# Reordering the matmuls, the copies and the DMA issues ahead of the scan in the mixer of a second block

## The reference, cut to what matters

```python
h = rms_norm(x, norm_mix_g);  p = h @ w_in
q, pc, pr = split(p)                       # 256, 768, 1536 columns
# memory attention: 4 heads of 64 over 256 rows kh, vh of the memory
s  = einsum('bqhd,bmhd->bhqm', qh, kh) * 64 ** -0.5
o_att = einsum('bhqm,bmhd->bqhd', softmax(s), vh)
# convolution: 31 taps along time for each of 384 channels, layer norm, silu
u = val * sigmoid(gate);  o_conv = silu(layer_norm(conv(u, conv_w) + conv_b))
# rwkv7, forward and backward: low-rank products for decay w, rate a, gate g
w = exp(-0.606531 * sigmoid(w0[d] + tanh(wd) @ decay_up[d]))      # rank 64, d = 0, 1
a = sigmoid(a0[d] + ad @ iclr_up[d])                              # rank 64, d = 0, 1
g = sigmoid(gd) @ gate_up                                         # rank 128
bonus[d] = sum(r * k_d * r_k, over a head's 64 channels) * v
state = state * w + (state @ -kk) (kk * a) + v k_d;  y = state @ r    # the scan
x = x + concat(o_att, o_conv, (group_norm(y) + bonus) * g) @ w_out
```

## Time and profile before

| what | value |
|---|---|
| time, median of 3 runs | 1654.49 us (1652.68 to 1655.73) |
| the profiled execution: span | 1657.7 us |
| PE busy, of the span | 1361.3 us (82%) |
| DVE, ACT, POOL busy | 423.9, 278.8, 128.0 us |
| mean granted clock of TensorE | 0.896 |
| chain that ended last, by engine | PE 53%, DMA 41% |

### The profile page before, as it was taken

The page is one execution under the profiler, slowest core; times in us unless marked ns, Lnnn a source line. Parts: engine busy times, 40 slices in busy tenths (PEclk is TensorE's granted clock), DMA queues, the critical chain, the costliest instruction groups (busy, mean ns, idle before and its releaser), DMA issues.

```text
span 1657.7 us, 26953 instructions
## 1 busy us (share of the span) xinstructions
PE 1361.3 (82%) x11688; PEld 766.4 (46%) x11688; DVE 423.9 (26%) x892; ACT 278.8 (17%) x626; POOL 128.0 (8%) x276
## 2 busy tenths in 40 slices
PE   5999999999999877877778689887987577566775
PEld 4756876787763323322223278676432122122221
DVE  1012135531273222222222244653520000000001
ACT  0201213551011111110111113331111100000001
POOL 4000013000000000000000004112000000000000
PEclk9999989999999999889898889967988878787679
DMA  9865381466469999999999691300979999999997
GB/s 347 269 171 208 110 299 57 166 238 238 178 254 396 426 429 427 429 429 429 427 429 427 288 330 51 95 3 4 375 313 429 428 429 427 430 428 428 428 428 308
DMA packets 86933, 513.90 MB, mean 310 GB/s; under 512 B 8969, under 2 KB 13498, under 8 KB 62274
## 3 DMA queue, kind: packets, MB, share of 16 engines
q1 hardware_dynamic: 82306, 502.84, 74.6%
q0 software_dynamic: 3872, 9.19, 2.3%
q10 hardware_dynamic: 672, 0.65, 0.2%
HBM read 507.77 MB, written 3.15 MB: 308 GB/s over the span
## 4 chain that ended last, share of the span: by engine, by line
PE 53%; DMA 41%; DVE 2%; issue 2%; ACT 1%; SPq 1%; POOL 0%; DVEq 0%; POOLq 0%; ACTq 0%
PE ps L1406 42%; DMA ring<-in_exp_w 19%; DMA arena<-in_w_e_down 19%; PE ps L2171 4%; DMA ring<-in_w_e_up 2%; PE ps L1495 2%; DMA ring<-in_w_in 1%; PE ps L1943 1%; PE ps L2371 0%; PE ps L1630 0%; SPq L621 0%; PE ps L1626 0%; DVE stats L2530 0%; PE ps L2183 0%; PE ps L1450 0%
## 5 line engine op out<-in xcount | busy, mean ns | idle before, releaser
L1406 PE MATMUL ps<-ring,arena 128*32 128x512 f32 (+4 forms) x1844 | 269.0, 656 | 102.7 <-DMA ring<-in_exp_w 86.3
L1406 PE MATMUL ps<-ring,hTs 128*32 128x512 f32 (+3 forms) x1056 | 231.3, 619 | 33.3 <-DMA ring<-in_w_e_up 19.5
L1406 PE MATMUL ps<-hTs,ring 128*128 128x256 f32 (+2 forms) x992 | 215.1, 384 | 0.1
L1406 PEld LDWEIGHTS ps<-ring,arena 128*32 128x32 f32 (+1 forms) x1844 | 85.9, 131 | 265.3 <-issue 243.1
L1406 PEld LDWEIGHTS ps<-hTs,ring 128*128 128x128 f32 (+2 forms) x992 | 185.0, 189 | 26.9 <-issue 1.6
L1406 PE MATMUL ps<-arena,vv 128*32 128x512 f32 (+2 forms) x560 | 94.7, 728 | 86.4 <-DMA arena<-in_w_e_down 82.0
L1406 PEld LDWEIGHTS ps<-ring,hTs 128*32 128x32 f32 (+1 forms) x1056 | 88.0, 140 | 150.9 <-issue 112.7
L1406 PE MATMUL ps<-arena,hTs 128*32 128x512 f32 x480 | 92.6, 621 | 0.0
L1406 PEld LDWEIGHTS ps<-arena,vv 128*32 128x32 f32 (+2 forms) x560 | 28.3, 144 | 137.3 <-DMA arena<-in_w_e_down 88.7
L2907 DVE COPY hTs<-ps 64x512 f32<-64x512 f32 x32 | 22.2, 693 | 260.4 <-PE ps L1406 260.4
L1136 ACT COPY arena<-ps 128x512 f32<-128x512 f32 x32 | 18.8, 586 | 389.4 <-PE ps L1921 389.4
(11 more groups left out here) (461 smaller groups left out, 1418.4 us busy)
## 6 DMA issues: line engine op xcount, KB each, us to landing
ring<-in_exp_w SPq DMA_DIRECT2D x92, 2048.0 KB, 22.0
arena<-in_w_e_down SPq DMA_DIRECT2D x28, 2048.0 KB, 25.7
ring<-in_w_e_gate SPq DMA_DIRECT2D x24, 2048.0 KB, 30.8
ring<-in_w_e_up SPq DMA_DIRECT2D x24, 2048.0 KB, 35.8
ring<-in_w_in SPq DMA_DIRECT2D x22, 2048.0 KB, 19.4
ring<-in_ada_w SPq DMA_DIRECT2D x12, 2048.0 KB, 16.1
arena<-in_w_e_up SPq DMA_DIRECT2D x8, 2048.0 KB, 34.3
arena<-in_w_e_gate SPq DMA_DIRECT2D x8, 2048.0 KB, 32.5
```

The source lines that it names most:

```text
L1406: return nc.tensor.matmul(o, lhsT, rhs, start=start, stop=stop)
```

## The change

The low-rank products go in rounds over the three column blocks, `w0` beside `w1` and `a0` beside `a1`, so that row halves alternate; all banks of a round's jobs are started first. The memory scores do the same with even and odd heads, and `mweigh` alternates column halves within a pair of heads. The job `qa` moves ahead of `bon` (in the plan and in TensorE's program). Of the 16 shifted copies SP issues eight instead of ten, ACT eight instead of six, and ACT issues them ahead of `decays(0, 1)` instead of behind it. The number of instructions on each engine stays as it was, but for the two issues that move.

```diff
-         ("kks", 1), ("vt", 2), ("ca", 1), ("kkb", 2), ("bon", 2), ("qa", 1), ("matt", 14),
+         ("kks", 1), ("vt", 2), ("ca", 1), ("kkb", 2), ("qa", 1), ("bon", 2), ("matt", 14),
...
             sp.wait_ge(S("cu_ready"), 1)
-            for j, q in LAGS[0:10]:
+            for j, q in LAGS[0:8]:
...
             frees(nc.scalar.copy(CA[:, 0:2, :], v3(bank(J("ca")), 2)), J("ca"))
-            decays(0, 1)
             act.wait_ge(S("cu_ready"), 1)
-            for j, q in LAGS[10:16]:
+            for j, q in LAGS[8:16]:
                 nc.scalar.dma_start(lags[32 * j:32 * j + 32, q::4, :], CU[32 * q:32 * q + 32, :, j:j + 284])\
                     .then_inc(S("lags_loaded"), 16)
+            decays(0, 1)
             is_full(act, J("qa"))
...
-            for name, m, rows, src in (("w0", 0, slice(0, 64), 9), ("w1", 0, slice(64, 128), 9), ("gg", 2, slice(0, P), 11),
-                                       ("a0", 1, slice(0, 64), 10), ("a1", 1, slice(64, 128), 10)):
-                for i in range(2):
-                    j = job(name, i)
-                    for c in range(2 * i, min(3, 2 * i + 2)):
-                        ins = mm(bank(j)[:, (c % 2) * 256:(c % 2) * 256 + 256], up2[rows, m, c * P:(c + 1) * P],
-                                 PF[rows, src, :])
-                    fills(ins, j)
+            def low_products(names, m, src):
+
+                js = [[job(name, i) for i in range(2)] for name in names]
+                rows = (slice(0, 64), slice(64, 128)) if len(names) == 2 else (slice(0, P),)
+                for c in range(3):
+                    for j, r in zip(js, rows):
+                        ins = mm(bank(j[c // 2])[:, (c % 2) * 256:(c % 2) * 256 + 256], up2[r, m, c * P:(c + 1) * P],
+                                 PF[r, src, :])
+                        if c > 0:
+                            fills(ins, j[c // 2])
+
+            low_products(("w0", "w1"), 0, 9)
+            low_products(("gg",), 2, 11)
+            low_products(("a0", "a1"), 1, 10)
...
+            products(job("qa"), slot(n, (8, 512)), 0, hT)
             pe.wait_ge(S("bonus_terms"), 4)
             block_sums("bon", BON)
-            products(job("qa"), slot(n, (8, 512)), 0, hT)
...
-            def mscore(h):
-                j = start(jM(f"S{h}"))
-                r = slice(64 * (h % 2), 64 * (h % 2) + 64)
-                for t in range(TT):
-                    ins = mm(v3(bank(j), TT)[:, t, :], qa[r, h // 2, t * P:(t + 1) * P], kmT[r, h // 2, :])
-                fills(ins, j)
+            def mscores(i):
+
+                js = [start(jM(f"S{h}")) for h in (2 * i, 2 * i + 1)]
+                for t in range(TT):
+                    for j, r in zip(js, (slice(0, 64), slice(64, 128))):
+                        ins = mm(v3(bank(j), TT)[:, t, :], qa[r, i, t * P:(t + 1) * P], kmT[r, i, :])
+                        if t:
+                            fills(ins, j)
...
-                for h in (2 * i, 2 * i + 1):
-                    for m in range(TT):
+                for m in range(TT):
+                    for h in (2 * i, 2 * i + 1):
...
-            for h in range(4):
-                mscore(h)
+            for i in range(2):
+                mscores(i)
```

## The result

| | before | changed |
|---|---|---|
| time, median of 20 runs each | 1654.72 us (1649.82 to 1662.67) | 1661.54 us (1656.46 to 1669.26) |
| ratio | | 1.0043, 95% interval 1.0031 to 1.0055 |
| profiled execution: span (time) | 1657.7 us | 1665.8 us (1667.65) |

The change makes the kernel slower: 6.8 us between the medians, a ratio of 1.0043 whose interval means +5.1 to +9.1 us. The prediction had +1.0 us and "no change that could be told".

A forecast was written before the change was run, and what follows sets the result against it. The prediction took TensorE's work and expert-weight transfers as the chain, with TensorE setting the mixer's pace. Its terms summed to -0.3 us, plus 1.3 for the clock: +1.0, 1655.5 us, range 1652.6 to 1657.4.

The forecast's parts named there:

- What bounds the stage: Mixer ahead of the scan: TensorE sets the pace, but copies land near the scores' end; faster TensorE alone gains almost nothing.
- Low-rank products and scores: On TensorE: alternating halves cut low-rank products from 5.6 to 3.94 us and scores from 2.16 to 1.80, saving 1.6 and 0.35.
- POOL: POOL starts 0.4 us earlier at best, so CU is ready at 1037.2 instead of 1037.65 and sets the copies' clock.
- The held queue: ACT's eight issues at 0.79 us hold decays and the query copy; scores start at 1045.9, TensorE waits 2.5 us.
- The clock: The 2.5 us wait ahead of the scores drops TensorE's granted clock to half, costing up to 1.65 us, 1.3 on average.
- Rival 3: Issues stretch to 0.94 us, TensorE waits 3.7 us, clock down for two stretches: +4.2 us, 1658.7 us; chance 0.10.
- The copies: Ahead of the convolution: last copy lands by 1046.7, the weight tile slowing copies by some tenths; copies off the path.
- the convolution waits for copies: At the convolution's start: a sign that would show the prediction wrong, since scores were to end at 1047.7, after the copies.
- The range: Whole kernel time: 1652.6 to 1657.4 us; 0.87 chance of staying within 3.3 us of no change.
- its base: Whole kernel: the median of 1654.49 us before the change, to which each predicted change was added.

The follow-up runs named there:

- decays first and tile held: Changed kernel with decays(0, 1) back ahead of ACT's eight issues, and SP's 2 MB weight tile waiting for all 16 copies: ratio 1.0000 to before, mixer 37.14 us.
- the first profile: Profile of the changed kernel, no further edit, from its first set of runs: mixer 42.43 us, ratio 1.0043 to the kernel before.
- the second: Profile of the changed kernel run once more without edit: mixer 41.64 us, ratio 1.0031 to the kernel before.
- tile held: Changed kernel, but SP sends the 2 MB weight tile only once all 16 shifted copies have landed: ratio 1.0016 to before, mixer 40.08 us.
- filling matmuls: Changed kernel with six more matmuls on TensorE between bonus sums and the wait for the queries: ratio 1.0027 to before, mixer 41.17 us.
- the queues' part, tile held: Kernel before with eight and eight issues, ACT's ahead of decays(0, 1), and the weight tile waiting for all copies: ratio 1.0004, mixer 38.74 us.
- the queues' part alone: Kernel before with only eight and eight issues, ACT's ahead of decays(0, 1): ratio 1.0013, mixer 42.53 us.

## Why the prediction was wrong, point by point

- **What bounds the stage.** Right for the chain. "A faster TensorE alone would have bought almost nothing" holds for the swap, which gained nothing. The low-rank part alone gained 1.14 us of mixer, but its copies landed 1.1 us earlier as well, which the prediction had not foreseen; with the copies where they were, the gain is 0.1 by my estimate above.
- **Low-rank products and scores.** 4.49 us, not 3.94, and 1.93 (where the clock holds: 1045.27 - 1043.34, decays first and tile held), not 1.80. Saved: 1.1 and 0.1 to 0.2, not 1.6 and 0.35. The rate was taken from records of 512 columns; these have 256 and did not reach half time.
- **POOL.** CU was ready 0.13 us earlier, not 0.4: POOL started 0.5 earlier, but its steps up to the end of CU took 10.4 us instead of 10.0, while DVE's slow steps lie elsewhere beside them than before; whether those are the reason was not tried.
- **The held queue.** Right: ACT's instructions wait for its issues. These took 0.84 each where 0.79 was taken, so the scores started 0.6 us later than before, not 0.05. The hole was 2.57 where 2.5 was forecast, and DVE's part 1 idled 1.79.
- **The clock.** Right in kind, from rows of another stage; +1.64 with the copies in time, where +1.3 was taken. In the first profile it stayed down 6.8 us and in the second 3.4. Rival 3 had the two stretches, for another reason.
- **The copies: the step that failed.** "The first weight tile now follows on SP at 1043.4 and may slow them by some tenths ... the copies are off the path." It slowed ACT's last copy by 3 to 4 us and put it on the path in every kernel that had eight and eight with the tile free. The prediction saw that the tile moves up behind the two issues that went away, but priced it without a row and left it out of the sum: a transfer of 2 MB, larger than all 16 copies together (16 x 106.5 KB), whose condition the swap had met earlier too. ACT's last copy landed after 6.9 to 8.0 us with the tile free, against at most 3.7 with it held, and with what it added to the clock's time it cost the changed kernel's mixer 1.6 to 2.4 us. That "the convolution waits for copies" was one of the prediction's own signs of being wrong. The section of the Trainium skill that I quoted for the issue time (DMA: Bandwidth & Descriptors, "Issuing engines are not separate DMA queues") also says that transfers of all issuing engines run on the same 16 DMA engines and interleave. The trace agrees, with both queues moving packets in the same microsecond (25 and 7), and it was the half that mattered.
- **The range.** It ended at 1657.4 us, +2.9 on its base; the mixer alone was +3.6 and +4.4. With the tile held, that is without the late copy, the mixer is +2.0 and the time +2.6, inside the range. The late copy was not among the bounds: the copies had their landing of before, 3.5 to 3.9, as if nothing else ran on the DMA engines. The rest of the 6.8 us, 2.4 to 3.2, no run explains.

## What to carry to other kernels

When DMA issues move from one queue to another, list what stands behind them on both: the compute instructions on the queue that gets them, and the next transfer on the queue that loses them. A large prefetch whose data is not needed for long goes behind a wait for the small transfers that are. And a hole that an edit opens ahead of dense matmuls can cost more than its own length, since the granted clock may fall with it (here in five profiles out of six with a hole of 2.17 us or more in this part).

## What the runs showed of the hardware that was not expected

- A 106.5 KB copy from SBUF to SBUF on ACT's queue, issued 0.8 to 1.5 us ahead of a 2 MB load on SP's queue, landed after 6.9 to 8.0 us in five profiles, against 3.9 at most for every other copy; the load itself landed 8.0 to 9.9 us after its issue.
- It was never more than the last copy on the other queue. In the same five profiles SP's own last copy, issued 0.8 to 1.7 us ahead of the load on the load's own queue, landed after 3.2 to 3.4 us. Whether a copy moved to SP's queue would be safe from the load was not tried as such.
- The clock did not fall with every hole: one of 2.57 us ahead of the convolution (filling matmuls) left it at 1.00, and so did one of 1.70 ahead of the scores (the queues' part, tile held); one of 2.56 us ahead of the scores (tile held) was followed by 3.4 us at 0.50, and so was one of 2.17 ahead of the convolution behind another of 1.57 (the queues' part alone).
- One issue of the same copy on SP took 0.61 us at the median in some kernels and 0.68 to 0.84 in others; what sets it was not tried.
